# First projection tile of a decoder trunk computed in two token halves, with its weight tile loaded between token tiles of x

## What is computed

```python
h = rms_norm(x, norm_pre_mix)          # x: 512 x 1024
proj = h @ w_in                        # rwkv | nsa | swa | gate columns
merged = sum(gate_b * (mixer_b(proj) @ w_branch[b]) for b in range(3))
x = x + rms_norm(merged @ w_out, norm_post_mix)
h = rms_norm(x, norm_pre_ffn)
out = x + rms_norm((silu(h @ ffn_w_gate) * (h @ ffn_w_up)) @ ffn_w_down, norm_post_ffn)
```

## Time and profile before

| | us |
|---|---|
| median of 3 runs (lowest, highest) | 1001.81 (1001.74, 1001.84) |
| the profiled execution: its time | 1001.6 |
| the profiled execution: its span in the trace | 999.8 |
| TensorE busy | 983.0 (98%) |
| VectorE / ScalarE / GpSimd busy | 692.9 / 425.5 / 452.3 |

### The profile page before, as it was taken

One profiled execution on the slowest core, in us unless ns is written; L12 is line 12 of the kernel. 1 busy time (PEld: TensorE's weight loads), 2 busy tenths in 40 slices (PEclk: granted clock), 3 DMA queues, 4 the chain that ended last, 5 costly groups with the idle time before them and its releaser, 6 DMA issues.

```text
span 999.8 us, 19627 instructions
## 1 busy us (share of the span) xinstructions
PE 983.0 (98%) x7920; PEld 799.7 (80%) x7920; DVE 692.9 (69%) x1160; ACT 425.5 (43%) x829; POOL 452.3 (45%) x511
## 2 busy tenths in 40 slices
PE   6999999999999999999999999999999999999997
PEld 5787777777777777777778888888889998888886
DVE  3799796565566956546556882269887865489987
ACT  4134432322314334546555444545444443345563
POOL 3366557254334766656683448446222234510000
PEclk9999999999999999999999999999999999999999
DMA  9345533122223564112113636433322333244452
GB/s 262 89 129 151 122 92 68 24 65 65 67 66 98 157 159 137 49 50 56 52 54 122 193 116 229 131 127 106 106 85 86 112 106 109 86 136 170 157 176 99
DMA packets 149459, 111.48 MB, mean 112 GB/s; under 512 B 21190, under 2 KB 132048, under 8 KB 149369
## 3 DMA queue, kind: packets, MB, share of 16 engines
q1 hardware_dynamic: 145644, 104.16, 35.7%
q10 hardware_dynamic: 3692, 6.07, 2.2%
q0 software_dynamic: 32, 0.00, 0.0%
HBM read 99.70 MB, written 10.52 MB: 110 GB/s over the span
## 4 chain that ended last, share of the span: by engine, by line
PE 86%; DVE 10%; issue 1%; DMA 1%; POOL 1%; ACT 1%; SPq 0%; DVEq 0%; ACTq 0%
PE ps L2318 33%; PE ps L2798 5%; PE ps L2797 5%; PE ps L2802 5%; PE ps L2332 4%; PE ps L2438 3%; PE ps L2683 3%; PE ps L2858 2%; PE ps L2860 2%; PE ps L2859 2%; PE ps L2625 2%; PE ps L2835 2%; PE ps L2832 2%; PE ps L2831 2%; DVE XF L1430 2%
## 5 line engine op out<-in xcount | busy, mean ns | idle before, releaser
L2318 PE MATMUL ps<-HLO,WHI 128*128 128x512 f32 x440 | 178.2, 405 | 0.4 <-issue 0.4
L2318 PE MATMUL ps<-HHI,WHI 128*128 128x512 f32 x440 | 175.5, 399 | 1.0 <-DVE HLO L1462 0.7
L773 POOL TENSOR_TENSOR WLO<-WRAW,WHI 128x1024 fp32r<-128x1024 f32 (+1 forms) x52 | 104.2, 2006 | 106.5 <-ACT WHI L888 106.5
L869 POOL TENSOR_TENSOR WLO<-WRAW,WHI 128x512 fp32r<-128x512 f32 x50 | 72.3, 1453 | 118.8 <-ACT WHI L1230 117.5
L2318 PE MATMUL ps<-HHI,WLO 128*128 128x512 f32 x440 | 118.1, 398 | 0.0
L777 POOL CAST WHI<-WRAW 128x256 fp32r<-128x256 f32 (+1 forms) x133 | 62.7, 472 | 106.5 <-PE ps L2318 106.3
L808 POOL TENSOR_TENSOR WLO<-WRAW,WHI 128x256 fp32r<-128x256 f32 x132 | 105.6, 800 | 10.7
L2318 PEld LDWEIGHTS ps<-HHI,WHI 128*128 128x128 f32 x440 | 82.6, 188 | 23.2 <-issue 4.7
L2318 PEld LDWEIGHTS ps<-HLO,WHI 128*128 128x128 f32 x440 | 82.6, 188 | 22.7 <-issue 5.1
L2318 PEld LDWEIGHTS ps<-HHI,WLO 128*128 128x128 f32 x440 | 80.5, 188 | 18.3 <-issue 1.4
L2798 PE MATMUL ps<-HLO,WHI 128*128 128x512 f32 x200 | 77.9, 389 | 0.0
(11 more groups left out here) (517 smaller groups left out, 2404.1 us busy)
## 6 DMA issues: line engine op xcount, KB each, us to landing
WRAW<-in_w_in SPq DMA_DIRECT2D x47, 512.0 KB, 4.4
WRAW<-in_w_gate SPq DMA_DIRECT2D x22, 512.0 KB, 3.8
WRAW<-in_w_up SPq DMA_DIRECT2D x22, 512.0 KB, 3.9
WRAW<-in_w_down SPq DMA_DIRECT2D x19, 512.0 KB, 3.4
spilled<-SQ SPq DMA_DIRECT2D x24, 256.0 KB, 2.4
GATES<-spilled SPq DMA_DIRECT2D x6, 768.0 KB, 4.8
WRAW<-in_w_in SPq DMA_DIRECT2D x16, 256.0 KB, 3.7
WRAW<-in_w_branch SPq DMA_DIRECT2D x32, 128.0 KB, 2.9
```

The source lines that it names most:

```text
L773: return pool.tensor_tensor(lo[:, 0:chunks, :], WRAW[:, n % NRAW, 0:chunks, :], hi[:, 0:chunks, :].bitcast(F32), ALU.subtract)
L869: pool.tensor_tensor(lo, raw_half(item[1], item[2]), hi.bitcast(F32), ALU.subtract).then_inc(w_lo, 1)
L2318: last = pe.matmul(DB[g % 2][:, :], (wlo if which == "low" else whi)[:, c, :], lo if which == "x_low" else hi, start=a == 0, stop=a == 3 * ...
```

## The change

- SP issues x tile 0, x tile 1, weight tile 0, x tile 2, x tile 3, weight tile 1. (Before: x 0, 1, 2, weight 0, x 3, weight 1.)
- GpSimd, not ScalarE, makes the high part of weight tile 0 too.
- The work on x and on job 0 is cut into two halves h of 256 tokens. Two chunks, k and k + 4, of one half share a PSUM bank (`x_chunk`): banks 2 to 5 for half 0, banks 6, 7, 1, 2 for half 1. ScalarE makes HHI in 16 pieces of 256 tokens, VectorE HLO in 16. ScalarE waits, for chunk k < 4, for the transposes of both chunks in the bank, and for k >= 4 for VectorE's piece of chunk k - 4.
- TensorE: transposes of x tile 0; of the parameters (into bank 0), ahead of x tile 1's; of x tile 1; the ten KEEP_BUSY transposes; high products of half 0, chunks 0 to 4; transposes of x tile 2; high products of chunks 5 to 7; transposes of x tile 3; low products of half 0; all products of half 1. That is 48 matmuls over 256 columns in place of 24 over 512.
- VectorE copies the parameters before it takes the squares of x tile 1. ScalarE takes the squares of x tile 2 after all of HHI.

```diff
--- before.py
+++ after.py
@@ -139,7 +139,7 @@
 NRAW, NSPL = 4, 2
 
 PIECE0 = NS0 + 5
-POOL_HI = [1]
+POOL_HI = [0, 1]
 KEEP_BUSY = 10
 
 SPILLED = list(range(SW0, GC0))
@@ -497,6 +497,9 @@
     psum = [nc.alloc_psum_tensor(f"ps{n}", [P, T], F32) for n in range(8)]
     DB, R = psum[0:2], psum[2:8]
     DB4 = [DB[0], DB[1], R[0], R[1]]
+
+    def x_chunk(h, k):
+        return psum[((2, 3, 4, 5), (6, 7, 1, 2))[h][k % 4]][:, 256 * (k // 4):256 * (k // 4) + 256]
 
     def head_cols(n, jj, sink=0):
         w = keys_of(n) + sink
@@ -676,10 +679,11 @@
             def x_tile(t):
                 sp.dma_start(XTOK0[:, t, :], x[t * P:(t + 1) * P, :]).then_inc(x_in[t], 16)
 
-            for t in range(3):
-                x_tile(t)
+            x_tile(0)
+            x_tile(1)
             for n in range(FF0):
                 if n == 1:
+                    x_tile(2)
                     x_tile(3)
                 if n == 2:
                     sp.dma_start(HOT[:, :], hot).then_inc(hot_in, 16)
@@ -896,12 +900,13 @@
 
             x_square(0)
             act.wait_ge(xsq_ok, 1)
+            act.wait_ge(prow_ok, 2)
+            for h in range(2):
+                for k in range(KC):
+                    act.wait_ge(*((xT_done, KC * h + 2 * k + 2) if k < 4 else (xlo_ok, KC * h + k - 3)))
+                    act.activation(HHI[:, k, 256 * h:256 * h + 256], x_chunk(h, k), ACT.Identity,
+                                   scale=par("g_pre_mix", k)).then_inc(xhigh_ok, 1)
             x_square(2)
-            hi_part(0)
-            act.wait_ge(prow_ok, 2)
-            for k in range(KC):
-                act.wait_ge(xT_done, k + 1)
-                act.activation(HHI[:, k, :], psum[k][:, :], ACT.Identity, scale=par("g_pre_mix", k)).then_inc(xhigh_ok, 1)
             act.wait_ge(xsq_ok, 2)
             act.wait_ge(xsum_ok, 2)
             act.activation(XRINV, XSS, ACT.Sqrt, scale=1.0 / D, bias=EPSC[:, 0:1]).then_inc(norm_std, 1)
@@ -1452,15 +1457,17 @@
                 dve.tensor_tensor_reduce(TMP[:, 0:2, :].rearrange("p a t -> p (a t)"), XTOK0[:, t, :], XTOK0[:, t, :],
                                          1.0, 0.0, ALU.mult, ALU.add, XSS[:, t:t + 1]).then_inc(xsum_ok, 1)
 
+            dve.wait_ge(prow_T, 1)
+            dve.tensor_copy(PARC[:, 0:NPAR1], DB[0][:, 0:NPAR1]).then_inc(prow_ok, 1)
+            dve.tensor_copy(PARC[:, NPAR1:NPAR1 + NPAR2], DB[0][:, P:P + NPAR2]).then_inc(prow_ok, 1)
             x_square(1)
-            dve.wait_ge(prow_T, 1)
-            dve.tensor_copy(PARC[:, 0:NPAR1], R[5][:, 0:NPAR1]).then_inc(prow_ok, 1)
-            dve.tensor_copy(PARC[:, NPAR1:NPAR1 + NPAR2], R[5][:, P:P + NPAR2]).then_inc(prow_ok, 1)
             dve.wait_ge(prow_ok, 2)
-            for k in range(KC):
-                dve.wait_ge(xhigh_ok, k + 1)
-                dve.scalar_tensor_tensor(out=HLO[:, k, :], in0=psum[k][:, :], scalar=par("g_pre_mix", k),
-                                         in1=HHI[:, k, :].bitcast(F32), op0=ALU.mult, op1=ALU.subtract).then_inc(xlo_ok, 1)
+            for h in range(2):
+                for k in range(KC):
+                    cols = slice(256 * h, 256 * h + 256)
+                    dve.wait_ge(xhigh_ok, KC * h + k + 1)
+                    dve.scalar_tensor_tensor(out=HLO[:, k, cols], in0=x_chunk(h, k), scalar=par("g_pre_mix", k),
+                                             in1=HHI[:, k, cols].bitcast(F32), op0=ALU.mult, op1=ALU.subtract).then_inc(xlo_ok, 1)
             dve.wait_ge(xsum_ok, 1)
             x_square(3)
             dve.wait_ge(norm_std, 1)
@@ -2279,10 +2286,6 @@
             def products_of(n):
 
                 ks = range(JOBS[n][3])
-                if n == 0:
-                    late = [("low", k - 2) for k in range(2, len(ks) + 2)]
-                    early = [[("x_high", k), ("x_low", k)] for k in ks]
-                    return early[0] + early[1] + sum(([late[k - 2]] + early[k] for k in ks[2:]), []) + late[-2:]
                 return [(part, k) for k in ks for part in ("x_high", "x_low")] + [("low", k) for k in ks]
 
             def steps(count):
@@ -2309,10 +2312,6 @@
                         for a in range(3 * k, 3 * k + 3):
                             which, c = order[a]
                             hi, lo = rhs(n, c)
-                            if n == 0 and which == "x_low":
-                                pe.wait_ge(xlo_ok, c + 1)
-                            if n == 0 and which == "x_high":
-                                pe.wait_ge(*((xhigh_ok, c + 1) if c else (xlo_ok, 1)))
                             if a == first_low:
                                 pe.wait_ge(w_lo, n + 1)
                             last = pe.matmul(DB[g % 2][:, :], (wlo if which == "low" else whi)[:, c, :],
@@ -2334,25 +2333,51 @@
 
             pe.wait_ge(con_in, 16)
             def x_transpose(t, k):
-                return tr(psum[k][:, t * P:(t + 1) * P], XTOK0[:, t, k * P:(k + 1) * P])
-
-            for t in range(3):
-                pe.wait_ge(x_in[t], 16)
-                for k in range(KC - 1):
-                    x_transpose(t, k)
+                at0 = P * (t % 2)
+                return tr(x_chunk(t // 2, k)[:, at0:at0 + P], XTOK0[:, t, k * P:(k + 1) * P])
+
+            def first_high(h, k):
+                cols = slice(256 * h, 256 * h + 256)
+                pe.wait_ge(xhigh_ok, KC * h + k + 1)
+                pe.matmul(DB[0][:, cols], split_of(0)[0][:, k, :], HHI[:, k, cols], start=k == 0, stop=False)
+                pe.wait_ge(xlo_ok, KC * h + k + 1)
+                pe.matmul(DB[0][:, cols], split_of(0)[0][:, k, :], HLO[:, k, cols], start=False, stop=False)
+
+            def first_low(h, k):
+                cols = slice(256 * h, 256 * h + 256)
+                return pe.matmul(DB[0][:, cols], split_of(0)[1][:, k, :], HHI[:, k, cols], start=False, stop=k == KC - 1)
+
+            pe.wait_ge(x_in[0], 16)
+            for k in range(KC):
+                x_transpose(0, k)
             pe.wait_ge(par_in, 32)
-            tr(R[5][:, 0:NPAR1], PRAW[0:NPAR1, 0, :], NPAR1)
-            tr(R[5][:, P:P + NPAR2], PRAW[0:NPAR2, 1, :], NPAR2).then_inc(prow_T, 1)
+            tr(DB[0][:, 0:NPAR1], PRAW[0:NPAR1, 0, :], NPAR1)
+            tr(DB[0][:, P:P + NPAR2], PRAW[0:NPAR2, 1, :], NPAR2).then_inc(prow_T, 1)
+            pe.wait_ge(x_in[1], 16)
+            for k in range(KC):
+                x_transpose(1, k // 2 + 4 * (k % 2)).then_inc(xT_done, 1)
             for n in range(KEEP_BUSY):
-                tr(psum[n % (KC - 1)][:, 3 * P:4 * P], ident)
+                tr(x_chunk(1, n % 3)[:, 0:P], ident)
+            pe.wait_ge(w_hi, 1)
+            pe.wait_ge(prow_ok, 2)
+            for k in range(5):
+                first_high(0, k)
+            pe.wait_ge(x_in[2], 16)
+            for k in range(KC):
+                x_transpose(2, k)
+            for k in range(5, KC):
+                first_high(0, k)
             pe.wait_ge(x_in[3], 16)
-            for k in range(KC - 1):
-                x_transpose(3, k).then_inc(xT_done, 1)
-            pe.wait_ge(prow_ok, 2)
-            for t in range(4):
-                last = x_transpose(t, KC - 1)
-            last.then_inc(xT_done, 1)
-            steps(8)
+            for k in range(KC):
+                x_transpose(3, k // 2 + 4 * (k % 2)).then_inc(xT_done, 1)
+            pe.wait_ge(w_lo, 1)
+            for k in range(KC):
+                first_low(0, k)
+            for k in range(KC):
+                first_high(1, k)
+                last = first_low(1, k)
+            last.then_inc(dense_done, 1)
+            dense["n"] = 1
             steps(4)
             pe.wait_ge(diag_ok, 4)
             pe.matmul(R[4][:, :], ones, SSUM[:, :], start=True, stop=True).then_inc(norm_ss, 1)
```

## The result

The changed kernel takes 1003.7 us (median of 21 runs, 1000.66 to 1005.23), against 1001.81 for the kernel before on the same chip (21 runs, 1001.14 to 1002.97). The ratio is 1.0018, with a 95% interval of 1.0012 to 1.0024: some 1.9 us slower. The forecast was 1001.1, its range ended at 1002.7. The profiled execution of the changed kernel took 1003.27 us, its span is 1001.5.

The account below looks back on a forecast made before the run. TensorE was taken to bound the kernel (86% of the chain), waiting at the head for x tile 3. Job 1 0.9 us sooner, less 0.2 for the cast, gave 1001.81 - 0.7 = 1001.1, range 999.9 to 1002.7.

Parts of the forecast that it names:

- P: Head: time at which the parameters are in, on which all of half 0 hangs; taken as 8.7, between 7.9 and 9.25.
- Rivals 1 and 2: Head: parameters land no sooner, P = 9.25, 1001.8 (chance 0.23); or with x tile 1, P = 7.9, 1000.1 (0.13).
- The meeting on VectorE and GpSimd: Head: VectorE's squares of x tile 1 slowed by GpSimd's cast of weight tile 0; between 0 and 0.8 us, taken as 0.2.
- TensorE's need at 12.1: Head: latest start of TensorE's ten matmuls of chunks 0 to 4, which need the cast's high part.
- rival 3: Head: TensorE stays at 1.2 GHz for longer, so slower, up to 1003.8; chance 0.17, of which 0.07 beyond 2 us slower.
- b: Head: time at which TensorE's clock level rises from 1.2 to 2.4 GHz.
- The formula: Head: eighteen transposes must be through at 12.1, which holds for b = 10.9; each us beyond costs 0.45.
- the sum: Whole kernel: job 1 starts 0.9 us sooner, less 0.2 for the meeting with the cast, gives 0.7 us gained.
- What it gains passes on as long as nothing behind it is tied to a fixed time: Behind the head: job 1's earlier start, 19.6 against 20.50, reaches the end unless something there has a fixed time.
- Rival 4: 24 to 100 us: the shift isn't passed on or meets another VectorE and GpSimd phase; some tenths either way, chance 0.05.
- The halves: Head: eight HLO pieces of 256 tokens take 3.23, eight HHI 3.03; HLO's second half starts near 15.9.
- the cases beyond: Whole kernel: outcomes slower by over 2 us, chance 0.08.

Follow-up runs that it names:

- the parameters later: Changed kernel with the parameters' transposes moved behind x tile 1's, and VectorE's copies behind its squares of x tile 1: 1001.29 us, ratio 1.0005.
- 12 tiny matmuls: Kernel before with 12 matmuls of 2 by 2 (48 instructions) in TensorE's idle time at the start: median 1001.27 us, ratio 1.0001.

## Why the prediction was wrong

*P, the parameters' landing: right.* 8.74 by the transfer's row, 8.78 by the transpose, against 8.7. Rivals 1 and 2 fell with it. The copies start at 9.58 (9.4 expected), HLO at 11.00, which is P + 2.2.

*The meeting on VectorE and GpSimd: wrong side.* I had 0.2 us for squares slowed by the cast. They take 1.22 as before, and the cast, which started 0.35 after them, takes 1.76 against 1.04 for the next one. With the parameters later, where the squares are done before the cast starts, it takes 1.03. The one that came first kept its speed. The cast ends at 11.97, ahead of TensorE's need at 12.1, so the price is 0.

*The level of TensorE, rival 3: the first step that failed, right in kind and wrong in chance.* "From P on, TensorE works for over 4 us without a break, so b beyond 13.5 is hard to see." Three executions had 12.34, 13.94 and 15.53. The formula itself holds: from 19.6 (the sum without the 0.2) and 0.45 us for each us beyond 10.9, job 1 should start at 20.25, 20.97 and 21.68; it did at 20.31, 21.13 and 21.89. The failed step is that I took the rise of one profile, before x tile 2, for a fixed property of the head, and put the loss by a later one at nothing in the sum. In three profiles of the old head with tiny matmuls the level rose at 12.22 to 12.42, with breaks of 0.54 to 0.61 us in front of x tile 1 and none like the changed head's 1.18, so the one profile was no ground for it. At the first profile's 12.34 the loss is 0.65 of the 0.9 expected; in the other two it is more than all of it. The mean of the three starts, 21.11, is 0.6 later than before. The new head is also more exposed: the late rise costs the old one 0.3 us.

*"What it gains passes on as long as nothing behind it is tied to a fixed time": the second step that failed, and the larger one in the first profile.* Nothing was tied to a time, but much is tied to a place in the program. Rival 4 had 0.05 and "some tenths either way"; it measured +1.89, -0.05 and +0.05 in three executions of the changed kernel, and +2.09, +2.33 and +2.87 for 48 instructions without the change. In the other executions it is often less: the median with 12 tiny matmuls did not move. The sum had this term at nothing. The three profiles side by side (the sums come out by construction, to the rounding of span against time; what is measured is how they divide):

| execution | head | behind | sum | measured, against 1001.6 |
|---|---|---|---|---|
| after | -0.19 | +1.89 | +1.70 | +1.67 |
| after, second | +1.39 | -0.05 | +1.34 | +1.32 |
| after, third | +0.63 | +0.05 | +0.68 | +0.66 |

*The halves.* The pieces took what I had said (HLO 3.22 and 3.23 for eight), and HLO's second half started at 16.54, not 15.9, which is the clock's 0.65 again. Squares of x tile 3, DIAG and the norm matmul caused no wait, as expected.

*The range.* It ended at 1002.7, since the cases beyond held 0.08 together. Two terms that the sum had at nothing came at once, and they add.

## What to carry to other kernels

Count the instructions that a change adds to an engine, not only their time: where an engine runs short instructions densely, a change anywhere ahead can move the borders of its instruction loads into or out of these stretches. In the profiles here that was worth from 2.9 us lost to 1.3 us won, more than the change itself, so a small difference is only read rightly beside a control whose program has the same length, and from many executions: one profile of the kernel with 48 idle instructions showed 2.3 us lost, and its median none. Beside a control of equal length no form of the changed head showed a gain that can be told. And before work is put behind a wait at the head, look at whether the engine idles there at its lower clock; filling that gap with work that was to be done anyway brought job 1 forward by 0.6 to 0.7 us.

## What the hardware showed that I had not expected

- An increment of a semaphore on TensorE as an instruction of its own costs some 0.15 us: 48 of them put the first transpose at 8.28, 100 at 16.21, 7.93 us for 52 more.
- TensorE idles for up to 1.15 us (in one run 1.74) at the border of a 16 KB packet of its instructions, and goes on 2.1 to 2.7 us after that packet's start. In these groups 64 matmuls with their loads, 128 instructions, take some 1.3 us (before, from 172.69 to the next matmul at 174.00), so 256 would take some 2.6, no more than those 2.1 to 2.7. Among long matmuls, at 0.23 us each, 256 instructions last 29 us. Both are estimates from these rows; that this ratio is the cause is argued, not shown.
- The same kernel raised TensorE's level at 12.34, 13.94 and 15.53 in three executions, although its work up to 11.2 started at the same times to 0.2 us (parameter transposes at 8.78, 8.97 and 8.90). The old head did so at 9.21, and with tiny matmuls ahead of it at 12.22, 12.42 and 12.35.
- VectorE's squares beside GpSimd's cast: the one that started later paid, 1.76 against 1.04, and VectorE nothing.
